# The scaling of the turned x: VectorE, one block ahead, in place of GpSimd

## The reference

```python
h = rmsnorm(x, g_pre)                    # x * rsqrt(mean(x*x) + eps) * g_pre
proj = h @ w_in                          # 2048 x 20496, columns split into q k v o za ig fg u vb zb ga gb
ig, lf = ig_pre + b_ig, log_sigmoid(fg_pre + b_fg)
# mLSTM over q, k, v with gates ig, lf: cumulative sums and a running maximum over the rows -> y_a
vb_n = layernorm(vb, ln_g, ln_b)
y_b = u * (tril(W_s) @ vb_n + b_s) * silu(zb)
merged = sigmoid(ga) * (y_a @ w_pa) + sigmoid(gb) * (y_b @ w_pb)
y = x + rmsnorm(merged @ w_out, g_post)
```

## Time and profile before

| | us |
| --- | --- |
| median of 3 runs | 1467.81 (1467.41 to 1467.86) |
| the profiled execution's own time | 1467.71 |
| its span | 1466.2 |
| PE busy in the span | 1446.1 (99%) |
| DVE, ACT, POOL busy | 880.7, 625.8, 212.6 |

### The profile page before, as it was taken

The page is one execution under the profiler, slowest core; times in us unless marked ns, Lnnn a source line. Parts: engine busy times, 40 slices in busy tenths (PEclk is TensorE's granted clock), DMA queues, the critical chain, the costliest instruction groups (busy, mean ns, idle before and its releaser), DMA issues. The chain is left out here.

```text
span 1466.2 us, 31047 instructions
## 1 busy us (share of the span) xinstructions
PE 1446.1 (99%) x11045; PEld 1424.2 (97%) x11045; DVE 880.7 (60%) x1472; ACT 625.8 (43%) x890; POOL 212.6 (15%) x360
## 2 busy tenths in 40 slices
PE   9899999999999999999999999999999999999996
PEld 8899999999999999999999999999999999999996
DVE  7876655564443447676767676767767544545444
ACT  6444433333333334444445454545454433333442
POOL 4500000002000000404141414141312000000000
PEclk9999999999999999999999999999999999999998
DMA  8475655557555568596969696969696665655553
GB/s 246 119 229 155 177 166 161 162 153 232 183 182 173 180 181 223 158 305 170 298 178 294 183 296 178 292 179 297 173 297 159 218 182 176 177 179 186 173 159 141
DMA packets 311285, 292.13 MB, mean 199 GB/s; under 512 B 82928, under 2 KB 297528, under 8 KB 310608
## 3 DMA queue, kind: packets, MB, share of 16 engines
q1 hardware_dynamic: 292080, 242.99, 58.4%
q0 software_dynamic: 19088, 48.58, 9.9%
q10 hardware_dynamic: 80, 0.07, 0.0%
HBM read 266.12 MB, written 25.44 MB: 199 GB/s over the span
## 5 line engine op out<-in xcount | busy, mean ns | idle before, releaser
L1091 DVE TENSOR_TENSOR wlo<-raw,whi 128x1024 fp32r<-128x1024 f32 x416 | 506.9, 1222 | 503.8 <-ACT whi L827 501.5
L827 ACT ACTIVATE whi<-raw 128x1024 fp32r<-128x1024 f32 x416 | 439.2, 1058 | 667.0 <-PE ps L460 638.7
L458 PE MATMUL ps<-xh,whi 128*128 128x288 f32 x2304 | 683.2, 297 | 0.0
L459 PE MATMUL ps<-xl,whi 128*128 128x288 f32 x2304 | 682.0, 296 | 0.0
L460 PE MATMUL ps<-xh,wlo 128*128 128x288 f32 x2304 | 679.0, 295 | 0.0
L458 PEld LDWEIGHTS ps<-xh,whi 128*128 128x128 f32 x2304 | 433.5, 188 | 4.8 <-issue 2.5
L459 PEld LDWEIGHTS ps<-xl,whi 128*128 128x128 f32 x2304 | 433.1, 188 | 0.4
L460 PEld LDWEIGHTS ps<-xh,wlo 128*128 128x128 f32 x2304 | 432.8, 188 | 0.0
L458 PE MATMUL ps<-yh,whi 128*128 128x288 f32 x768 | 228.1, 297 | 0.6 <-DVE yl L1110 0.6
L459 PE MATMUL ps<-yl,whi 128*128 128x288 f32 x768 | 227.6, 296 | 0.0
L460 PE MATMUL ps<-yh,wlo 128*128 128x288 f32 x768 | 226.6, 295 | 0.0
(11 more groups left out here) (362 smaller groups left out, 1047.3 us busy)
## 6 DMA issues: line engine op xcount, KB each, us to landing
raw<-in_w_in_dram SPq DMA_DIRECT2D x320, 512.0 KB, 3.9
raw<-in_w_pb_dram SPq DMA_DIRECT2D x32, 512.0 KB, 3.5
Cin<-in_state_mlstm_C_dram POOLq DMA_DIRECT2D x16, 1024.0 KB, 8.5
Xb<-in_state_mlstm_C_dram SPq DMA_DIRECT2D x256, 64.0 KB, 3.7
out_dram<-Cin POOLq DMA_DIRECT2D x16, 1024.0 KB, 6.1
raw<-in_w_pa_dram SPq DMA_DIRECT2D x32, 512.0 KB, 3.5
raw<-in_w_out_dram SPq DMA_DIRECT2D x32, 512.0 KB, 3.5
bcs<-rows_d POOLq DMA_DIRECT2D x8, 304.0 KB, 3.7
```

What stands on the lines that cost most here:

```text
L458: nc.tensor.matmul(out, whi[:, c, kk, cols], mh_[:, k, :], start=(k == 0), stop=False)
L459: nc.tensor.matmul(out, whi[:, c, kk, cols], ml_[:, k, :], start=False, stop=False)
L827: nc.scalar.activation(whi[:, c], raw[:, c], ACT.Copy).then_inc(hi_ready, 1)
L1091: nc.vector.tensor_tensor(wlo[:, c], raw[:, c], whi[:, c].bitcast(F32), ALU.subtract).then_inc(lo_ready, 1)
```

## The change

POOL no longer multiplies. DVE does it with the same 16 operations (`scaled_x`): block 0 after pair 3's work, and block k + 1 right behind the `split_lo` that belongs to block k, ahead of `from_turned` where there is one. `x_ev` is now counted by DVE. The hardware loop over pairs 4 to 7 on DVE becomes a loop in Python, written out.

```diff
+        def scaled_x(k):
+            nc.vector.tensor_tensor(xT[:, k, :], xT[:, k, :], r_row[:], ALU.mult).then_inc(x_ev, 1)
...
                     if scale:
                         lower_x(k)
                     split_lo(V0 + 1 + s + 2 * i, c)
+                    if scale and k + 1 < KT:
+                        scaled_x(k + 1)
                     if c == 1 and (s, c, 0) not in small:
                         from_turned(1 - s, 2 * i + s - 1, 2 * PW * i + PW * (s - 1))
...
-        with dve.Fori(2, 4) as i:
+        scaled_x(0)
+        for i in (2, 3):
             v_body(i, scale=True)
...
         pool.wait_ge(x_var, 1)
         nc.gpsimd.tensor_tensor(rx[:], stat[:], half[:], ALU.pow).then_inc(x_rstd, 1)
-        pool.wait_ge(r_step, 4)
-        for k in range(KT):
-            nc.gpsimd.tensor_tensor(xT[:, k, :], xT[:, k, :], r_row[:], ALU.mult).then_inc(x_ev, 1)
         pool.wait_ge(g_rows, 1)
```

## The result

The changed kernel takes 1472.25 us (median of 8 runs, 1471.61 to 1472.78) against 1468.18 for the kernel before (8 runs on the same chips, 1467.41 to 1469.22): a ratio of 1.0027, 95% interval 1.0016 to 1.0037. It is slower by 4.1 us, or 0.28%. The profiled executions, 1472.78 and 1467.71, lie at the slow and the quick end of these, so that the two traces differ by 5.1 us.

A forecast was written before the change was run, and what follows sets the result against it. PE was taken as the bound, busy 1446.1 of 1466.2 us. Pair 8 starting 1.2 us later plus 1.05 for the clock gave +2.3 on 1467.71: 1470.0 us, range 1466.4 to 1472.8.

The forecast's parts named there:

- the stall in pair 3: PE's wait for `vf` in pair 3: 5.1 us, plus 1.4 at low clock behind it, both forecast to go.
- the ring: ACT's `xh` and `whi`, DVE's `wlo` and multiplication form a cycle: 3.06 us a turn, 43.2 over 13 turns.
- the door of pair 8: PE's entry into pair 8, waiting for `xl`: forecast at 134.6 in place of 133.41, 1.2 us later.
- Part 1: The multiplications leave POOL: DVE's gates chain in pair 3 takes 4.62 us against 9.44, 4.82 saved.
- The shift: Everything on DVE, ACT and POOL that hangs on the gates chain comes 6.1 us earlier, bounds 5.1 to 6.8.
- Rival (c): The ring is dearer by 0.1 a turn, or the load 1 us later: 1471 to 1472.3 us; chance 0.25.
- PE's stalls: PE's wait is moved, not removed: some 2 us at the turn in pair 5, 5.5 before pair 8.
- The clock: Low clock around pair 8's start, after PE's wait there: costs 1.05 us, bounds 0 and 1.4.
- (a): The ring is late by less: pair 8 at 132.3, 1466.6 or 1467.7 us, down to 1463; chance 0.13.
- (b): DVE's gates chain is slow by itself, so the stall in pair 3 stays: +8.3, 1476 us; chance 0.05.

The follow-up runs named there:

- matmuls filled in: The changed kernel with 24 idle matmuls of 128 columns on PE just ahead of its wait for `xl` before pair 8: 1470.52 us, ratio 1.0014.
- late rows: The changed kernel with bsb, lng and lnb loaded only when block 4's `xl` is written: 1469.85 us, ratio 1.001 to the kernel before.
- two blocks ahead: The changed kernel with DVE's multiplication of block k + 2, not k + 1, behind the `split_lo` of block k: 1461.81 us, ratio 0.996.

## Why the prediction was right, and where its sizes were not

The forecast was 1470.0 with a range of 1466.4 to 1472.8, and 0.56 on "no change" against 0.36 on "slower by over 0.2%". The measured time lies in the range, and the result is on the slower side of that bound. Its interval, 1.0016 to 1.0037, takes that bound in. The mechanism was right: the stall in pair 3 went, the ring formed and kept its late start, and PE waited for `xl` at the door of pair 8 at a fallen clock. The sum of +2.3 us came out as +4.1 by the medians and +5.1 by the traces, and the narrower forecast, 1468.2 to 1471.0 with a chance of 0.55, was missed. That the time still lies in the range is in part luck: the range was widened for a dearer ring, and more than half of the excess came from the clock, which no rival priced above 1.4. Term by term:

- **Part 1.** The chain without POOL took 63.46 - 58.74 = 4.72 us, forecast 4.62; the start was forecast at 58.72, a scan at 0.75 and came at 0.74; POOL's lng issue at 72.06, forecast 72.0. The stall went. That POOL's work was what slowed the chain is shown by putting it back. By the rule that the Trainium skill gives in "SBUF — State Buffer", "Who interferes with whom", a DVE instruction with two SBUF inputs and a GpSimd instruction that reads SBUF contend for the shared port pair, and the one issued second waits for the whole of the other. The rows agree with it: 1.05 and 0.44 for one instruction, with POOL busy and idle.
- **The shift.** Forecast 6.1 us for everything behind the chain; the issues did come 6.1 sooner, but the first `xh` and pair 5's chunk 2 only 5.7 (86.83 to 81.11, 96.73 to 91.03), as the DMAs took longer to land: 0.4 late. This looks like scatter of the loads: counted from PE's turn in pair 2, that chunk's `whi` comes after 38.5 us here (52.51 to 91.03), and after 37.7 and 37.8 in the two variants with the same work up to there (matmuls filled in, ACT's loop written out).
- **The ring.** The sum of 43.2 us from block 2 to block 15 took 135.19 - 91.03 = 44.2. The term that was sized wrongly is the hand-over from DVE to ACT. I took it as 0.04 from a wait on a constant; ACT waits for `x_ev` in a hardware loop, with a register operation in between, and it took 0.13 to 0.14. Rival (c) named this very cause, with 0.1 a turn. ACT's loop written out brings 0.04 back and takes 1.2 us off pair 8's start. So the loop is shown to be the cause; that it is the register operation in it is not shown by itself.
- **The door of pair 8.** 135.83 in place of 134.6: 0.4 from the shift, 1.0 from the ring, less 0.2, as `xl` came sooner behind `xh` than I had it. That is the same effect the other way: from the end of `xh` to `xl` it took 0.20 in DVE's loop before (86.83 + 0.44 to 87.47), and 0.03 now that this loop is written out; in the kernel before with only that loop written out it took 0.04. The 1.2 are beyond the 0.6 us from which rival (c) decides for "slower".
- **PE's stalls.** Forecast: 2 us at the turn in pair 5, 5.5 before pair 8. Measured 2.7 and 4.6. The first is longer by the 0.4 of the load, 0.1 of the ring, and the time from ACT's copy to the turn, 0.93 and not 0.73 (95.16 to 96.09). I hadn't reckoned with the clock falling in between, which kept PE busy for 1.5 us more and so shortened the second.
- **The clock.** Forecast 1.05, with 1.4 as the upper bound, since I took the low stretch before for its length. It lasted twice as long in the changed kernel (134.9 to 141.7) and cost 2.7, outside my bounds. This is the largest error of the sum, 1.6 of the 2.8 us by which the trace exceeds it; the other 1.2 are the door of pair 8. The matmuls filled into the wait take it back at that place.
- Rivals (a) and (b) did not come. Of (a) the start of the ring was tested: an earlier start does move pair 8 one for one, but not far enough to make the change gain.

## What to carry to other kernels

When a helper step is moved between engines, draw the ring that it closes: who waits for it, what stands ahead of it in its new queue, and what that waits for. If one turn of the ring is as long as the bound engine's own pace, every lateness at its start is kept to the end; one position earlier in the queue (here ahead of `wlo`, or one block sooner) is worth more than the engine on which the step runs. And a short chain of dependent small instructions is the wrong place for another engine's bulk work beside it: moving GpSimd's 16 multiplications 21 us later alone gave 0.4%.

## What the runs showed of the hardware

- The same wait of PE is followed by low-clock stretches of different length. The kernel before had one of 3.4 us with a wait of 4.93; the same program with VectorE's loop written out had, after the same wait, one from about 67.7 to 74.5:

```profile
67.00:68.00 1.00, 0.00 (x0) 0.00 (x0) 0.96 (x2) 0.00 (x0) 1.00 (x2) 0.85 0.00 0
74.00:75.00 1.00, 1.00 (x8) 1.00 (x7) 0.95 (x5) 0.00 (x0) 0.00 (x0) 0.74 0.82 163
```

  It began 2.0 us after PE's last matmul had ended, not 4.3, and cost 1.9 us, not 1.4 (to PE's turn in pair 4 it took 86.64 - 70.60 = 16.0 us and 86.43 - 70.89 = 15.5, against 79.99 - 65.81 = 14.2 in the changed kernel, at full clock). Over all traces of this stage five such stretches lasted 3.4 us and four 6.8, behind waits of 1.9 to 5.3 us.
- Part of the spread of a kernel's runs fits this. Of the 27 runs of the kernel before in one session, the six with the highest mean clock (0.996) took 1467.3 to 1467.9 us, and the four with the lowest (0.994) 1468.5 to 1469.5. But it can't be all of it: the runs spread over 3.7 us with the late rows, where PE waits 5.3, and also over 3.4 with the matmuls filled in and 4.3 with two blocks ahead, whose profiled executions have no low clock in this stage. What else moves them is open.
- A wait of 1.9 us was followed by a fallen clock in one execution (ACT's loop written out, 96.8 to 100.2), and by none in another (with the matmuls filled in), nor was one of 1.7 (GpSimd's work put back); waits of 0.7 us or less in this stage never were.
- A semaphore from DVE took 0.04 us to start a waiting ACT instruction in straight code, and 0.13 to 0.14 in a hardware loop. From ACT to DVE it was 0.03 to 0.04 and about 0.2.
